# Reordering the opening of a two-block transformer kernel: the first token half ahead of the second, on one Trainium2 core

## Chip, cores and metric

The kernel runs on one core of one Trainium2 chip. The metric is the device time of one execution in microseconds (us), less is better. Engine names: PE is TensorE (matrix products; PEld its weight loads), DVE is VectorE, ACT is ScalarE, POOL is GpSimd, SP is SyncE, which issues most DMA transfers here.

## What is computed

Two blocks follow each other on x of 1024 tokens by 1024 channels, all in float32: a two-layer block (Fourier mixing and differential attention, then a short convolution, each with a modulated norm) and a second block (recurrent mixers and an MLP). Only the first modulated norm and the first projection bear on this change:

```python
m = jax.nn.silu(cvec) @ w + b
shift, scale, gate = jnp.split(m, 3, axis=-1)
h = rms_norm(x, g) * (1.0 + scale) + shift     # rms_norm: x / sqrt(mean(x*x) + 1e-6) * g
proj = h @ w_in
```

The rest of the reference (attention, convolutions, recurrences, the MLP) is the same work before and after.

## The kernel before

The program is written out by hand: one instruction list for each engine, tied together with semaphores, so each engine runs its instructions in the order written. Activations lie with channels on the 128 partitions, eight tiles of 128 channels (`k`), and 1024 tokens in the free dimension, which is handled as two halves of 512 (`h`). A projection unit is 128 output channels. Each product is made of three matmuls (high part by high, low part by high, high part by low): ACT rounds a weight tile to its high part (`Whi`, line 475), POOL subtracts to get the low part (`Wlo`, line 403), and PE multiplies.

The opening does the following.

- SP loads the parameters, then `x` as eight tiles of 512 KB (line 332: four for half 0, four for half 1), weight unit 0, two tiles of the modulation matrix `adaW` of 1 MB each (line 340), weight unit 1, then the other `adaW` tiles.
- ACT squares the 16 tiles of `x` (line 532), DVE adds them in fours (lines 1011, 1013, `add_fours`), PE sums over channels with a matrix of ones (line 1576), ACT takes the root (line 536), DVE inverts it (line 980, `root_to_scale`), giving `Rx` for each half.
- PE multiplies `silu(c)` by pairs of `adaW` tiles (line 1582, `modulation_rows(j)`, j from 0 to 3), ACT copies the result to `mrow` (line 540, `rows_out`), PE turns it into columns (line 1603, `modulation_columns(j)`), and DVE makes of them the shift `M` and the scale `A0` of two channel tiles (lines 990 to 995, its own `modulation_columns(j)`).
- For each channel tile and half, DVE makes the scaled tile `tnx` (line 1000, `scaled_half`), ACT adds the shift and rounds to the high part `Hh` (line 545, `high_half`), DVE makes the low part `Hl` (line 1005, `low_half`), and PE adds the tile's products to two units at once (lines 1614 to 1616, `first_products`: six matmuls a half).

On PE the order is: four sum matmuls, rows 0, columns 0, then for j = 1 to 3 the products of one half tile, rows j, one half tile, columns j, two half tiles, and at the end the last four half tiles. After that come the context's square sum (line 1637), the second pair of weights, and the projections that fill most of the kernel (lines 1489 to 1491).

Of the kernel before, what the change touches and what calls it, by code (L numbers as in the profile page):

```python
# [17 lines left out]
P = 128  # L18
# [4 lines left out]
KT = D // P  # L23
# [86 lines left out]
def build(nc, I, out_dram):  # L110
    names = {}

    def sem(name):
        if name not in names:
            names[name] = nc.alloc_semaphore(name)
        return names[name]
# [4 lines left out]
    def at(name, offset, shape, dt=F32):  # L121
        return nc.alloc_sbuf_tensor_at(name, [P] + list(shape), dt, offset=base + offset)
# [142 lines left out]
    def bank(b, n=512, off=0):  # L265
        return PS[:, b * 512 + off:b * 512 + off + n]
# [38 lines left out]
    def sp_program(sp):  # L305
# [20 lines left out]
        sp.dma_start(P12[:, :], nW["params"]).then_inc(sem("params_loaded"), 16)  # L326
        sp.dma_start(basic[:, :], nW["basic"]).then_inc(sem("const_loaded"), 16)
        xk = nW["x"].rearrange("p (k n) -> p k n", k=KT)
        for h in range(2):
            c = slice(h * 512, h * 512 + 512)  # L330
            for j in range(4):
                sp.dma_start(X[:, 2 * j:2 * j + 2, c], xk[:, 2 * j:2 * j + 2, c]).then_inc(sem(f"x_loaded{h}{j}"), 16)
        unit_at(0, 0, w_in0)
        for t in range(8):
            if t == 2:
                unit_at(1, P, w_in0)
            col = 1024 * (t % 2) + 256 * (t // 2)
            if t >= 4:
                sp.wait_ge(sem("ada_read"), t - 3)
            sp.dma_start(adaW[:, t % 4, :, :], ada[:, 0, :, col:col + 256]).then_inc(sem(f"ada_loaded{t % 4}"), 16)  # L340
        sp.wait_ge(sem("xsq_read"), 3)
        sp.dma_start(Xc[:, :, :], nW["ctx"].rearrange("p (k n) -> p k n", k=KT)).then_inc(sem("ctx_loaded"), 16)
        for u in range(2, BASE["g"] + 3):
# [126 lines left out]
    def act_program(act):  # L470
        def split(u, slot, load, tiles=KT):

            act.wait_ge(w_loaded[slot], load)
            act.wait_ge(acc_ready, u + 1)
            act.activation(Whi[:, slot, 0:tiles, :], Wraw[:, slot, 0:tiles, :], COPY).then_inc(hi_ready, 1)  # L475
# [48 lines left out]
        act.activation(small[:, 32:40], small[:, 24:32], ACT.Exp, scale=-1.0).then_inc(sem("lam_exp"), 1)  # L524
        act.wait_ge(sem("lamsum"), 1)
        act.activation(small[:, 8:10], bank(0, 2), ACT.Exp).then_inc(sem("lamexp"), 1)
        for n in range(2 * KT):
            h, k = n // KT, n % KT
            act.wait_ge(sem(f"x_loaded{h}{k // 2}"), 16)
            if n == 12:  # L530
                act.wait_ge(sem("xsq_read"), 1)
            act.activation(xsq[:, n % 12, :], X[:, k, h * 512:h * 512 + 512], SQUARE).then_inc(sem("xsq_ready"), 1)
        split(0, 0, 16)
        for h in range(2):
            act.wait_ge(sem("xsq_read"), 2 * h + 2)
            act.activation(Rx[:, h * 512:h * 512 + 512], bank(4 + h), SQRT, bias=EPSC, scale=1.0 / D).then_inc(sem("x_root"), 1)

        def rows_out(j):
            act.wait_ge(sem("ada_psum"), 2 * j + 2)
            act.activation(mrow[:, :, :], PS[:, 6 * 512:8 * 512].rearrange("p (t n) -> p t n", t=2)[:, :, 0:256], COPY).then_inc(sem("m_copied"), 1)  # L540

        def high_half(n):
            k, c = n // 2, slice(n % 2 * 512, n % 2 * 512 + 512)
            act.wait_ge(sem("x_tn"), n + 1)
            act.activation(Hh[:, k, c], tnx[:, n % 4, :], IDN, bias=M[:, k, 0:1]).then_inc(sem("x_hi"), 1)

        rows_out(0)
        split(1, 1, 16)
        act.dma_start(chan[:, :], nW["chan_dft"]).then_inc(sem("chan_loaded"), 16)
        for j in range(4):  # L550
            high_half(4 * j)
            high_half(4 * j + 1)
            if j < 3:
                rows_out(j + 1)
            high_half(4 * j + 2)
            high_half(4 * j + 3)
# [331 lines left out]
    def dve_program(dve):  # L888
# [88 lines left out]
        def root_to_scale(h):  # L977
            c = slice(h * 512, h * 512 + 512)
            dve.wait_ge(sem("x_root"), h + 1)
            dve.reciprocal(Rx[:, c], Rx[:, c])  # L980
            dve.drain()
# [14 lines left out]
            dve.drain().then_inc(sem("m_ready"), 1)  # L996

        def scaled_half(n):
            k, c = n // 2, slice(n % 2 * 512, n % 2 * 512 + 512)
            stt(tnx[:, n % 4, :], X[:, k, c], A0[:, k:k + 1], Rx[:, c], ALU.mult, ALU.mult).then_inc(sem("x_tn"), 1)  # L1000

        def low_half(n):
            k, c = n // 2, slice(n % 2 * 512, n % 2 * 512 + 512)
            dve.wait_ge(sem("x_hi"), n + 1)
            stt(Hl[:, k, c], tnx[:, n % 4, :], M[:, k, 0:1], Hh[:, k, c].bitcast(F32), ALU.add, ALU.subtract).then_inc(sem("x_lo"), 1)

        def add_fours(n):
            a = 4 * (n % 3)
            for b in (0, 2):
                dve.wait_ge(sem("xsq_ready"), 4 * n + b + 2)  # L1010
                tt(xsq[:, a + b, :], xsq[:, a + b, :], xsq[:, a + b + 1, :], ALU.add)
            dve.drain()
            tt(xsq[:, a, :], xsq[:, a, :], xsq[:, a + 2, :], ALU.add).then_inc(sem("xsq_added"), 1)

        for n in range(4):
            add_fours(n)
        root_to_scale(0)
        root_to_scale(1)
        modulation_columns(0)
        for j in range(4):  # L1020
# [9 lines left out]
            if j < 3:  # L1030
                modulation_columns(j + 1)
# [446 lines left out]
    def pe_program(pe):  # L1478
# [93 lines left out]
        for h in range(2):  # L1572
            for j in range(2):
                n = 2 * h + j
                pe.wait_ge(sem("xsq_added"), n + 1)
                mm(bank(4 + h), ones, xsq[:, 4 * (n % 3), :], start=(j == 0), stop=(j == 1)).then_inc(sem("xsq_read"), 1)

        def column_tiles(out, W, sem_done):

# [5 lines left out]
        def modulation_rows(j):  # L1585

            if j:
                pe.wait_ge(sem("m_copied"), j)
            for t in range(2):
                pe.wait_ge(sem(f"ada_loaded{(2 * j + t) % 4}"), 16 * (j // 2 + 1))  # L1590
                column_tiles(bank(6 + t, 256), adaW[:, (2 * j + t) % 4, :, :], "ada_psum")
                pe.drain().then_inc(sem("ada_read"), 1)

        def modulation_columns(j):

            pe.wait_ge(sem("m_copied"), j + 1)
            if j >= 2:
                pe.wait_ge(sem("m_ready"), j - 1)
            if j == 0:
                pe.wait_ge(sem("x_root"), 2)  # L1600
# [5 lines left out]
        def first_products(k, h):  # L1606

            pe.wait_ge(sem("x_lo"), 2 * k + h + 1)
            c = slice(h * 512, h * 512 + 512)
            for u in range(2):  # L1610
                if k == 0 and h == 0:
                    pe.wait_ge(lo_ready, u + 3)
                    pe.wait_ge(sem("lamexp"), 1)
                mm(acc(u)[:, c], Whi[:, u, k, :], Hh[:, k, c], start=(k == 0), stop=False)
                mm(acc(u)[:, c], Whi[:, u, k, :], Hl[:, k, c], start=False, stop=False)
                last = mm(acc(u)[:, c], Wlo[:, u, k, :], Hh[:, k, c], start=False, stop=(k == KT - 1))
                if k == KT - 1 and h == 1:
                    last.then_inc(acc_ready, 1)

        pe.wait_ge(sem("cs_ready"), 2)  # L1620
        modulation_rows(0)
        modulation_columns(0)
        for j in range(1, 4):
            first_products(2 * j - 2, 0)
            modulation_rows(j)
            first_products(2 * j - 2, 1)
            modulation_columns(j)
            first_products(2 * j - 1, 0)
            first_products(2 * j - 1, 1)
        for k in (6, 7):  # L1630
            for h in range(2):
                first_products(k, h)
        for k in range(KT):
            pe.wait_ge(sem("csq_ready"), k + 1)
            if k == 0:
# [463 lines left out]
```

## Time and profile before

| | |
|---|---|
| median of 3 runs | 2922.23 us (2921.93 to 2924.31) |
| profiled execution, its own time | 2921.74 us |
| span of its trace | 2919.9 us |
| PE busy | 2836.0 us, 97% of the span |
| DVE busy | 1436.9 us, 49% |
| ACT busy | 902.2 us, 31% |
| POOL busy | 636.3 us, 22% |

The span runs from the first to the last instruction; the execution's own time is 1.8 us longer. Starts in the trace are counted from the span's start. Of the span only about the first 45 us are in an order that the change touches.

### The profile page before, as it was taken

The numbers are of one execution on the slowest core, as the hardware profiler recorded it, in microseconds if no ns is written. First come the engines' busy times: TensorE is split into PE (matmuls) and PEld (weight loads), VectorE is DVE, ScalarE is ACT, GpSimd is POOL, SyncE is SP. The second block draws the span as 40 slices with busy tenths as digits, with TensorE's granted clock in tenths as the row PEclk, the third lists the DMA queues.
The fourth block names the chain that finished last, engine by engine and source line by source line (L and its number), as shares of the span: only waits on it lengthen the run. The fifth ranks groups of instructions, "written<-read, shape, count | busy, mean of one in ns | idle before, by whom it ended". The sixth has DMA issues, their size and how long they took to land.

```text
span 2919.9 us, 34652 instructions
## 1 busy us (share of the span) xinstructions
PE 2836.0 (97%) x14282; PEld 2360.1 (81%) x14282; DVE 1436.9 (49%) x1522; ACT 902.2 (31%) x1020; POOL 636.3 (22%) x348
## 2 busy tenths in 40 slices
PE   7999998899999999999999999999999999999997
PEld 4878777887788888788888888888877888888886
DVE  6478128877422226545555565655766213131236
ACT  4332226653211113444442222222333112121122
POOL 0111115214222213222221111111032121222222
PEclk9999999999999999999999999999999999999999
DMA  7211440023111112111111111111021111111113
GB/s 227 68 29 40 148 144 1 1 73 90 47 51 49 45 51 82 51 49 44 51 54 37 37 30 37 37 37 31 28 80 51 51 51 44 51 51 49 46 54 112
DMA packets 276868, 168.52 MB, mean 58 GB/s; under 512 B 5616, under 2 KB 270192, under 8 KB 276336
## 3 DMA queue, kind: packets, MB, share of 16 engines
q1 hardware_dynamic: 275280, 162.88, 19.0%
q10 hardware_dynamic: 1440, 3.51, 0.3%
q8 instruction: 113, 1.85, 0.3%
q14 instruction: 35, 0.29, 0.0%
HBM read 162.17 MB, written 4.19 MB: 57 GB/s over the span
## 4 chain that ended last, share of the span: by engine, by line
issue 52%; PE 36%; POOL 7%; DVE 2%; ACT 2%; DVEq 1%; POOLq 0%; ACTq 0%
PE PS L1489 10%; PE PS L1491 10%; PE PS L1490 10%; POOL Wlo L403 7%; ACT exp L677 1%; DVE acol L1159 1%; PE PS L1661 1%; DVEq L1163 1%; PE PS L1798 1%; PE PS L1582 1%; PE PS L1670 0%; PE PS L1801 0%; PE PS L1651 0%; PE PS L1681 0%; PE PS L1680 0%
## 5 line engine op out<-in xcount | busy, mean ns | idle before, releaser
L403 POOL TENSOR_TENSOR Wlo<-Wraw,Whi 128x1024 fp32r<-128x1024 f32 (+1 forms) x240 | 571.7, 2382 | 2113.2 <-ACT Whi L475 2113.2
L1489 PE MATMUL PS<-Bh,Whi 128*128 128x512 f32 x2176 | 860.6, 396 | 3.6 <-POOL Wlo L403 3.6
L1491 PE MATMUL PS<-Bh,Wlo 128*128 128x512 f32 x2176 | 849.6, 390 | 0.0
L1490 PE MATMUL PS<-Bl,Whi 128*128 128x512 f32 x2176 | 849.4, 390 | 0.0
L475 ACT ACTIVATE Whi<-Wraw 128x1024 fp32r<-128x1024 f32 (+1 forms) x240 | 250.4, 1043 | 781.5 <-PE PS L1491 779.1
L1489 PEld LDWEIGHTS PS<-Bh,Whi 128*128 128x128 f32 x2176 | 410.3, 189 | 91.8 <-POOL Wlo L403 6.5
L1491 PEld LDWEIGHTS PS<-Bh,Wlo 128*128 128x128 f32 x2176 | 409.9, 188 | 86.7
L1490 PEld LDWEIGHTS PS<-Bl,Whi 128*128 128x128 f32 x2176 | 410.3, 189 | 83.8 <-issue 1.5
L1489 PE MATMUL PS<-Hh,Whi 128*128 128x512 f32 x1120 | 444.8, 397 | 6.8 <-POOL Wlo L403 3.6
L1491 PE MATMUL PS<-Hh,Wlo 128*128 128x512 f32 x1120 | 437.5, 391 | 0.0
L1490 PE MATMUL PS<-Hl,Whi 128*128 128x512 f32 x1056 | 412.5, 391 | 0.0
L1489 PEld LDWEIGHTS PS<-Hh,Whi 128*128 128x128 f32 x1120 | 211.1, 188 | 59.1 <-issue 14.0
L1491 PEld LDWEIGHTS PS<-Hh,Wlo 128*128 128x128 f32 x1120 | 211.0, 188 | 44.5
L1490 PEld LDWEIGHTS PS<-Hl,Whi 128*128 128x128 f32 x1056 | 199.1, 189 | 42.0 <-issue 1.7
L1466 DVE TENSOR_TENSOR sq<-ut 128x1024 f32<-128x1024 f32 x32 | 83.7, 2616 | 197.0 <-ACT ut L880 197.0
L1473 DVE TENSOR_TENSOR X<-X,PS 128x1024 f32<-128x1024 f32 x24 | 29.3, 1221 | 214.3 <-PE PS L1491 214.3
L1933 PEld LDWEIGHTS PS<-hZ 128*128 128x128 f32 x896 | 108.8, 194 | 5.3 <-DVE hZ L1344 1.8
L1933 PE MATMUL PS<-hZ 128*128 128x64 f32 x896 | 107.8, 274 | 1.8 <-DVE hZ L1344 1.7
L1330 DVE COPY_PREDICATED hP<-mk,PS 128x512 f32<-128x512 int32 x56 | 50.1, 895 | 118.0 <-PE PS L1933 117.8
L677 ACT ACTIVATE exp<-PS,acol 128x1280 f32<-128x1280 f32 x60 | 79.6, 1327 | 60.3 <-DVE acol L1164 60.3
L910 DVE TENSOR_TENSOR sacc<-sacc,sqs 128x512 f32<-128x512 f32 x48 | 84.0, 1749 | 26.8 <-ACT sqs L494 26.8
L1825 PE MATMUL PS<-vT,probT 128*128 128x128 f32 x640 | 76.8, 275 | 0.0
(323 smaller groups left out, 3057.9 us busy)
## 6 DMA issues: line engine op xcount, KB each, us to landing
Wraw<-in_w_in SPq DMA_DIRECT2D x64, 512.0 KB, 4.1
Wraw<-in_w_down SPq DMA_DIRECT2D x38, 512.0 KB, 3.8
adaV<-in_ada_w SPq DMA_DIRECT2D x16, 1024.0 KB, 5.2
Wraw<-in_odd_w_in SPq DMA_DIRECT2D x32, 512.0 KB, 4.1
Wraw<-in_w_up SPq DMA_DIRECT2D x32, 512.0 KB, 4.1
Wraw<-in_even_w_in SPq DMA_DIRECT2D x24, 512.0 KB, 3.8
adaW<-in_ada_w SPq DMA_DIRECT2D x8, 1024.0 KB, 11.2
Wraw<-in_even_w_out SPq DMA_DIRECT2D x14, 512.0 KB, 3.8
```

The lines of the kernel that those rows point to most:

```text
L403: pool.tensor_tensor(Wlo[:, slot, 0:tiles, :], Wraw[:, slot, 0:tiles, :], Whi[:, slot, 0:tiles, :].bitcast(F32), ALU.subtract).then_inc(lo ...
L475: act.activation(Whi[:, slot, 0:tiles, :], Wraw[:, slot, 0:tiles, :], COPY).then_inc(hi_ready, 1)
L677: act.activation(weights_of(b, m)[:, :], PS[:, (S0, S1)[m]:(S0, S1)[m] + NK], ACT.Exp, bias=acol[:, b % 3, 5 + m:6 + m], accum_out=acol[:, ...
L910: tt(sacc[:, h, :], sacc[:, h, :], sqs[:, n % 2, :], ALU.add).then_inc(sem("sq_added"), 1)
L1330: dve.copy_predicated(hP[:, :].rearrange("p (c b two l) -> p c b two l", c=8, two=2, l=L)[:, :, :, 1, :], mk[lev][:, :].rearrange("p (a n) ...
L1466: tt(sq2[:, k % 2, :], ut[:, k % 2, :], ut[:, k % 2, :], ALU.mult).then_inc(sem("usq_ready"), 1)
L1473: tt(X[:, k, :], X[:, k, :], acc(k % 2), ALU.add).then_inc(acc_free[k % 2], 1)
L1489: mm(out, Whi[:, u % 2, k, :], hi[:, k, c], start=(k == 0), stop=False)
L1490: mm(out, Whi[:, u % 2, k, :], lo[:, k, c], start=False, stop=False)
L1491: return mm(out, Wlo[:, u % 2, k, :], hi[:, k, c], start=False, stop=(k == KT - 1))
L1825: ins = mm(rows_in(b), probT[:, b % 2, t, :], vT[:, t, h * P:(h + 1) * P], start=(t == 0), stop=(t == 9))
L1933: ins = mm(bank(4 + lev % 2, 64, c * 64).rearrange("p (b l) -> p b l", l=L), z, right, start=True, stop=True)
```

## The change

Tiles of `x` for half 0 are loaded first, then `adaW` tile 0, weight unit 0, `adaW` tile 1, weight unit 1, and only then half 1 of `x`. On ACT the root's table is loaded ahead of the squares by a root of one column whose result is not used, the squares of half 0 are followed by root 0, and the squares of half 1 stand behind the high parts of the first two tiles. On DVE and PE the sum, root and inversion of half 1 stand behind the first two half tiles, which are now channel tiles 0 and 1 of half 0 (`FIRST`) in place of both halves of tile 0. `modulation_rows(1)` stands behind half 1's sum, and `modulation_columns(1)` between the two half-1 tiles. The slots of the squares (`SQUARES_AT`) change so that those of half 1 do not meet `tnx`.

```diff
+    SQUARES_AT = (0, 4, 8, 4)
+    FIRST = [(0, 0), (1, 0), (0, 1), (1, 1)] + [(k, h) for k in range(2, KT) for h in range(2)]
...
-        unit_at(0, 0, w_in0)
-        for t in range(8):
-            if t == 2:
-                unit_at(1, P, w_in0)
+        x_half(0)
+        ada_tile(0)
+        unit_at(0, 0, w_in0)
+        ada_tile(1)
+        unit_at(1, P, w_in0)
+        x_half(1)
+        for t in range(2, 8):
+            ada_tile(t)
...
+        act.activation(small[:, 10:11], EPSC, SQRT)
...
+        for n in range(KT):
+            square(n)
+        x_root(0)
+        split(0, 0, 16)
         rows_out(0)
         split(1, 1, 16)
         act.dma_start(chan[:, :], nW["chan_dft"]).then_inc(sem("chan_loaded"), 16)
-        for j in range(4):
+        high_half(0)
+        high_half(1)
+        for n in range(KT, 2 * KT):
+            square(n)
+        x_root(1)
+        high_half(2)
+        rows_out(1)
+        high_half(3)
+        for j in range(1, 4):
...
-        for n in range(4):
-            add_fours(n)
+        add_fours(0)
+        add_fours(1)
         root_to_scale(0)
+        modulation_columns(0)
+        scaled_half(0)
+        scaled_half(1)
+        low_half(0)
+        low_half(1)
+        add_fours(2)
+        add_fours(3)
         root_to_scale(1)
-        modulation_columns(0)
-        for j in range(4):
+        scaled_half(2)
+        scaled_half(3)
+        low_half(2)
+        low_half(3)
+        for j in range(1, 4):
+            modulation_columns(j)
...
+        x_sum(0)
         modulation_rows(0)
         modulation_columns(0)
-        for j in range(1, 4):
-            first_products(2 * j - 2, 0)
+        first_products(0)
+        first_products(1)
+        x_sum(1)
+        modulation_rows(1)
+        first_products(2)
+        modulation_columns(1)
+        first_products(3)
+        for j in range(2, 4):
+            first_products(4 * j - 4)
             modulation_rows(j)
-            first_products(2 * j - 2, 1)
+            first_products(4 * j - 3)
             modulation_columns(j)
-            first_products(2 * j - 1, 0)
-            first_products(2 * j - 1, 1)
+            first_products(4 * j - 2)
+            first_products(4 * j - 1)
```

On PE, from the first six products on, this is the order before (`L1614` to `L1616` are products, `L1582` the `adaW` pieces, `L1603` the columns):

```order
L1614 MATMUL PS<-Hh,Whi 128x512 [waits lamexp,lo_ready]
L1615 MATMUL PS<-Hl,Whi 128x512
L1616 MATMUL PS<-Hh,Wlo 128x512
L1582 MATMUL PS<-adaW,cs 2x256 [waits ada_loaded2,m_copied]
L1582 MATMUL PS<-adaW,cs 2x256 x7
L1582 MATMUL PS<-adaW,cs 2x256 [waits ada_loaded3]
L1582 MATMUL PS<-adaW,cs 2x256 x7
L1614 MATMUL PS<-Hh,Whi 128x512 [waits x_lo]
L1615 MATMUL PS<-Hl,Whi 128x512
L1616 MATMUL PS<-Hh,Wlo 128x512
L1614 MATMUL PS<-Hh,Whi 128x512
```


and with the change, from the second half tile's products on (the same three product lines are now 1648 to 1650, the sum 1609, the `adaW` pieces 1615):

```order
L1648 MATMUL PS<-Hh,Whi 128x512
L1649 MATMUL PS<-Hl,Whi 128x512
L1650 MATMUL PS<-Hh,Wlo 128x512
L1609 MATMUL PS<-xsq,basic 128x512 [waits xsq_added] x2
L1615 MATMUL PS<-adaW,cs 2x256 [waits ada_loaded2,m_copied]
L1615 MATMUL PS<-adaW,cs 2x256 x7
L1615 MATMUL PS<-adaW,cs 2x256 [waits ada_loaded3]
L1615 MATMUL PS<-adaW,cs 2x256 x7
L1648 MATMUL PS<-Hh,Whi 128x512 [waits x_lo]
L1649 MATMUL PS<-Hl,Whi 128x512
L1650 MATMUL PS<-Hh,Wlo 128x512
```


Half 1's sum now stands between the second half tile and the `adaW` pieces of the second pair, so everything behind it on PE waits for half 1's squares and their additions.

On ACT, from half 1's squares on, the order before (line 532 squares, 536 roots, 540 the row copy, 475 the weights' high part, 545 `Hh`):

```order
L532 ACTIVATE xsq<-X 128x512 [waits x_loaded10] x2
L532 ACTIVATE xsq<-X 128x512 [waits x_loaded11] x2
L532 ACTIVATE xsq<-X 128x512 [waits xsq_read,x_loaded12]
L532 ACTIVATE xsq<-X 128x512 [waits x_loaded12]
L532 ACTIVATE xsq<-X 128x512 [waits x_loaded13] x2
L475 ACTIVATE Whi<-Wraw 128x1024 [waits acc_ready,w_loaded0]
L536 ACT_TABLE_LOAD
L536 ACTIVATE Rx<-PS,Dv 128x512 [waits xsq_read] x2
L540 ACTIVATE mrow<-PS 128x512 [waits ada_psum]
L475 ACTIVATE Whi<-Wraw 128x1024 [waits acc_ready,w_loaded1]
L549 DMA chan<-in_chan_dft 128x256
L545 ACTIVATE Hh<-tnx,M 128x512 [waits x_tn] x2
```


and with the change, from half 0's root on (now lines 543, 547, 551, 484 and 556):

```order
L547 ACTIVATE Rx<-PS,Dv 128x512 [waits xsq_read]
L484 ACTIVATE Whi<-Wraw 128x1024 [waits acc_ready,w_loaded0]
L551 ACTIVATE mrow<-PS 128x512 [waits ada_psum]
L484 ACTIVATE Whi<-Wraw 128x1024 [waits acc_ready,w_loaded1]
L564 DMA chan<-in_chan_dft 128x256
L556 ACTIVATE Hh<-tnx,M 128x512 [waits x_tn] x2
L543 ACTIVATE xsq<-X 128x512 [waits x_loaded10] x2
L543 ACTIVATE xsq<-X 128x512 [waits x_loaded11] x2
L543 ACTIVATE xsq<-X 128x512 [waits xsq_read,x_loaded12]
L543 ACTIVATE xsq<-X 128x512 [waits x_loaded12]
L543 ACTIVATE xsq<-X 128x512 [waits x_loaded13] x2
L547 ACTIVATE Rx<-PS,Dv 128x512 [waits xsq_read]
```


All eight squares of half 1 and its root now stand behind the first two `Hh` tiles, which wait for `tnx`; before, they stood ahead of the weights' high part and of both roots.

## Rows read from the trace of the kernel before

**Rows 1.** The page: span, and part 1, busy time of TensorE.

```profile
span 2919.9 us, 34652 instructions
...
PE 2836.0 (97%) x14282; PEld 2360.1 (81%) x14282; DVE 1436.9 (49%) x1522; ACT 902.2 (31%) x1020; POOL 636.3 (22%) x348
```

**Rows 2.** Timeline from 0 us, PE: start, duration, engine, line, operation, xcount, [idle before <-releaser].

```profile
18.70 2.08 PE L1576 MATMUL PS<-xsq,basic 128*128 128x512 f32 x2 [0.71 <-DVE xsq L1013]
...
20.87 1.89 PE L1582 MATMUL PS<-adaW,cs 128*2 128x256 f32 x16
...
23.84 1.89 PE L1582 MATMUL PS<-adaW,cs 128*2 128x256 f32 x16 [1.08 <-DMA adaW<-in_ada_w]
...
26.44 1.87 PE L1603 MATMUL PS<-P,mrow 128*128 128x2 f32 x8 [0.72 <-ACT mrow L540]
...
32.32 0.80 PE L1614 MATMUL PS<-Hh,Whi 128*128 128x512 f32 x1 [4.01 <-DVE Hl L1005]
...
35.18 3.33 PE L1582 MATMUL PS<-adaW,cs 128*2 128x256 f32 x32
...
38.66 0.49 PE L1614 MATMUL PS<-Hh,Whi 128*128 128x512 f32 x1
...
40.15 0.95 PE L1603 MATMUL PS<-P,mrow 128*128 128x2 f32 x8
...
44.18 0.50 PE L1614 MATMUL PS<-Hh,Whi 128*128 128x512 f32 x1 [0.20 <-DVE Hl L1005]
```

**Rows 3.** The same timeline, ACT.

```profile
6.18 0.17 ACT L526 ACTIVATE small<-PS 128x2 f32<-128x2 f32 x1 [0.60 <-PE PS L1571]
...
7.57 2.43 ACT L532 ACTIVATE xsq<-X 128x512 f32<-128x512 f32 x4 [0.18 <-DMA X<-in_x]
...
10.16 1.15 ACT L532 ACTIVATE xsq<-X 128x512 f32<-128x512 f32 x2 [0.17 <-DMA X<-in_x]
...
16.00 1.15 ACT L532 ACTIVATE xsq<-X 128x512 f32<-128x512 f32 x2 [0.28 <-DMA X<-in_x]
17.75 1.06 ACT L475 ACTIVATE Whi<-Wraw 128x1024 fp32r<-128x1024 f32 x1 [0.59 <-DMA Wraw<-in_even_w_in]
18.82 1.28 ACT L536 ACT_TABLE_LOAD   x1
...
20.11 1.39 ACT L536 ACTIVATE Rx<-PS,Dv 128x512 f32<-128x512 f32 x2
...
30.76 1.39 ACT L545 ACTIVATE Hh<-tnx,M 128x512 fp32r<-128x512 f32 x2 [3.43 <-DVE tnx L1000]
```

**Rows 4.** The same timeline, DVE.

```profile
20.83 6.78 DVE L980 RECIPROCAL Rx<-Rx 128x512 f32<-128x512 f32 x2 [2.19 <-ACT Rx L536]
...
28.35 0.16 DVE L990 TENSOR_TENSOR M<-PS,P 128x4 f32<-128x4 f32 x1 [0.73 <-PE PS L1603]
...
29.98 1.41 DVE L1000 SCALAR_TENSOR_TENSOR tnx<-X,Dv,Rx 128x512 f32<-128x512 f32 x2
...
41.16 0.15 DVE L990 TENSOR_TENSOR M<-PS,P 128x4 f32<-128x4 f32 x1
```

**Rows 5.** DMA issues from 20.76 to 23.6 us: KB, us from issue to landing.

```profile
adaW<-in_ada_w SPq DMA_DIRECT2D x1, 1024.0 KB, 11.2
```

**Rows 6.** Timeline from 50 us, PE: a later pass, and the end of the opening.

```profile
53.66 0.50 PE L1614 MATMUL PS<-Hh,Whi 128*128 128x512 f32 x1 [0.26 <-DVE Hl L1005]
...
74.68 0.47 PE L1489 MATMUL PS<-Hh,Whi 128*128 128x512 f32 x1 [2.33 <-POOL Wlo L403]
```

**Rows 7.** Windows, from 75.6 us, behind an idle time: busy times, then PEclk, DMA share, GB/s.

```profile
75.60:79.00 3.40, 3.40 (x10) 2.69 (x9) 3.32 (x6) 0.00 (x0) 2.13 (x1) 0.54 0.90 347
```

**Rows 8.** Windows: the stretch behind PE's longest idle time after 38 us.

```profile
444.98:448.40 3.42, 3.42 (x22) 2.32 (x23) 3.34 (x5) 2.02 (x2) 3.27 (x2) 1.00 0.00 0
```

**Rows 9.** Timeline of PE from 441 us: the idle time ahead of that stretch.

```profile
444.98 0.48 PE L1798 MATMUL PS<-kT,qT 64*128 64x256 f32 x1 [2.75 <-ACT exp L677]
```

**Rows 10.** Source line 1533 up to 700 us: ns of one, min/median/max, and starts.

```profile
L1533 PE MATMUL PS<-sacc,basic x2: 592/644/697, 697.4 to 697.9; 128*128 128x512 f32 x2
```

More of the change, by code:

```diff
@@ L328, in sp_program, with x_half @@
         xk = nW["x"].rearrange("p (k n) -> p k n", k=KT)
-        for h in range(2):
+        def x_half(h):
             c = slice(h * 512, h * 512 + 512)
@@ L332, in sp_program, with ada_tile @@
                 sp.dma_start(X[:, 2 * j:2 * j + 2, c], xk[:, 2 * j:2 * j + 2, c]).then_inc(sem(f"x_loaded{h}{j}"), 16)
-        unit_at(0, 0, w_in0)
-        for t in range(8):
-            if t == 2:
-                unit_at(1, P, w_in0)
+        def ada_tile(t):
             col = 1024 * (t % 2) + 256 * (t // 2)
@@ L526, in act_program, with square @@
         act.activation(small[:, 8:10], bank(0, 2), ACT.Exp).then_inc(sem("lamexp"), 1)
-        for n in range(2 * KT):
+        act.activation(small[:, 10:11], EPSC, SQRT)
+        def square(n):
             h, k = n // KT, n % KT
@@ L530, in act_program, with x_root @@
             if n == 12:
[L531 to L534, printed above, removed]
+                act.wait_ge(sem("xsq_read"), 2)
+            act.activation(xsq[:, SQUARES_AT[n // 4] + n % 4, :], X[:, k, h * 512:h * 512 + 512], SQUARE).then_inc(sem("xsq_ready"), 1)
+        def x_root(h):
             act.wait_ge(sem("xsq_read"), 2 * h + 2)
@@ L542, in high_half @@
         def high_half(n):
-            k, c = n // 2, slice(n % 2 * 512, n % 2 * 512 + 512)
+            k, c = FIRST[n][0], slice(FIRST[n][1] * 512, FIRST[n][1] * 512 + 512)
             act.wait_ge(sem("x_tn"), n + 1)
             act.activation(Hh[:, k, c], tnx[:, n % 4, :], IDN, bias=M[:, k, 0:1]).then_inc(sem("x_hi"), 1)
+        for n in range(KT):
+            square(n)
+        x_root(0)
+        split(0, 0, 16)
         rows_out(0)
@@ L998, in scaled_half @@
         def scaled_half(n):
-            k, c = n // 2, slice(n % 2 * 512, n % 2 * 512 + 512)
+            k, c = FIRST[n][0], slice(FIRST[n][1] * 512, FIRST[n][1] * 512 + 512)
             stt(tnx[:, n % 4, :], X[:, k, c], A0[:, k:k + 1], Rx[:, c], ALU.mult, ALU.mult).then_inc(sem("x_tn"), 1)
         def low_half(n):
-            k, c = n // 2, slice(n % 2 * 512, n % 2 * 512 + 512)
+            k, c = FIRST[n][0], slice(FIRST[n][1] * 512, FIRST[n][1] * 512 + 512)
             dve.wait_ge(sem("x_hi"), n + 1)
@@ L1007, in add_fours @@
         def add_fours(n):
-            a = 4 * (n % 3)
+            a = SQUARES_AT[n]
             for b in (0, 2):
@@ L1029, in dve_program @@
             low_half(n + 3)
-            if j < 3:
-                modulation_columns(j + 1)
         dve.wait_ge(sem("lam_exp"), 1)
@@ L1571, in pe_program, with x_sum @@
         mm(bank(0, 2), ones[0:64, :], small[0:64, 16:18], start=True, stop=True).then_inc(sem("lamsum"), 1)
-        for h in range(2):
+        def x_sum(h):
             for j in range(2):
@@ L1575, in pe_program @@
                 pe.wait_ge(sem("xsq_added"), n + 1)
-                mm(bank(4 + h), ones, xsq[:, 4 * (n % 3), :], start=(j == 0), stop=(j == 1)).then_inc(sem("xsq_read"), 1)
+                mm(bank(4 + h), ones, xsq[:, SQUARES_AT[n], :], start=(j == 0), stop=(j == 1)).then_inc(sem("xsq_read"), 1)
         def column_tiles(out, W, sem_done):
@@ L1598, in modulation_columns @@
                 pe.wait_ge(sem("m_ready"), j - 1)
-            if j == 0:
-                pe.wait_ge(sem("x_root"), 2)
+            if j < 2:
+                pe.wait_ge(sem("x_root"), j + 1)
             for t in range(2):
@@ L1604, in modulation_columns, with first_products @@
             ins.then_inc(sem("m_psum"), 1)
-        def first_products(k, h):
-            pe.wait_ge(sem("x_lo"), 2 * k + h + 1)
+        def first_products(n):
+            k, h = FIRST[n]
+            pe.wait_ge(sem("x_lo"), n + 1)
             c = slice(h * 512, h * 512 + 512)
@@ L1620, in pe_program @@
         pe.wait_ge(sem("cs_ready"), 2)
+        x_sum(0)
         modulation_rows(0)
         modulation_columns(0)
-        for j in range(1, 4):
-            first_products(2 * j - 2, 0)
+        first_products(0)
[7 more added lines that the diff above has]
+            first_products(4 * j - 4)
             modulation_rows(j)
-            first_products(2 * j - 2, 1)
+            first_products(4 * j - 3)
             modulation_columns(j)
-            first_products(2 * j - 1, 0)
-            first_products(2 * j - 1, 1)
-        for k in (6, 7):
-            for h in range(2):
-                first_products(k, h)
+            first_products(4 * j - 2)
+            first_products(4 * j - 1)
+        for n in range(12, 16):
+            first_products(n)
         for k in range(KT):
```

## Prediction

> **What bounds the kernel now.** Read the page first: PE is busy 2836.0 of 2919.9 us [rows 1], so the kernel ends when PE's list ends, and only PE's idle or slow time can be won. Then read the opening of the timeline. PE's first product stands at 32.32, after 4.01 us of idleness that ended with `Hl` [rows 2]. Followed back: `tnx` at 29.98 and the modulation columns at 28.35 [rows 4], the column turn at 26.44, and the second `adaW` tile, whose arrival at 23.84 ended a wait on DMA [rows 2]. So the first product hangs on that load. The inversions of both roots, 6.78 us from 20.83, end at 27.61, ahead of the columns at 28.35 [rows 4]: hidden. From 32.32 on PE is nearly gap free: two half tiles, `adaW` pieces and columns, up to the fifth half tile at 44.18, where it waited 0.20 us for `Hl` [rows 2]. The next like place is at 53.66 [rows 6], 9.48 us on, and the order from the fifth half tile on is unchanged. **So the change is worth what it moves that start from 44.18**; all behind it follows one for one, through the wait at 74.68 for POOL's `Wlo` [rows 6] too, since that tile's high part on ACT waits for the last product.
>
> **Part 1, loads.** Four `x` tiles are put behind the second `adaW` tile. ACT's squares start at 10.16 and 16.00 on the fourth and eighth tile's landing [rows 3]: 5.84 us of transfer. The second `adaW` tile then lands at 23.84 - 5.84 = 18.00. The bytes ahead of the third and fourth `adaW` tiles are the same as before, so the fourth still lands near 20.78 + 11.2 = 32 (issue and time to landing, [rows 5]); nothing later is late for its user.
>
> **Part 2, the first two half tiles.** The table load is moved ahead of the squares: 1.28 us [rows 3], from 6.35 (6.18 + 0.17) to 7.63, and a small root, about 0.1. Eight squares at 2.43 for four [rows 3] run from 7.75 to about 12.6; all their `x` has landed by 10.16. From the last square's end (16.00 + 1.15) to the last sum matmul at 18.70 it took 1.55 [rows 2, 3], so this sum starts at 14.15 and lasts 2.08 [rows 2], to 16.2. The first `adaW` tile's pieces follow, 1.89, to 18.15, so the second's start there and not at 18.00. The root (0.69) and one inversion (half of 6.78, 3.39) end near 20.4, hidden under this. The first product comes 8.48 us after the second `adaW` pieces (32.32 - 23.84), hence at **26.6; 5.7 us earlier than before**. The two `Hh` end at about 26.3 (32.15 before).
>
> What the trace shows of the table load: it lasts 1.28 us and the root starts at 20.11, 0.01 us behind its end, and the load itself starts straight after the work ahead of it [rows 3]. The Trainium skill, "ScalarE: Activation LUTs", section "What ACT_TABLE_LOAD costs", counts a drain of about 1380 ns more for every switch, 2.66 us in all. By that page the first sum and all behind it would come about 1.4 us later and the total would be 2927.8. The trace does not agree, and I use 1.28.
>
> **Part 3, the second half: a chain that was hidden.** Behind the second `Hh` (26.3) ACT makes eight squares, 4.8 us (twice 2.43), to 31.1; 1.55 to the last sum matmul: not before 32.65. PE has meanwhile done two half tiles: six products took 2.86 us (32.32 to 35.18) while PE ran at half rate, and 1.49 (38.66 to 40.15) at full rate [rows 2]. Both now start before PE is at full rate: 2.86, then six more 0.43 apart, 2.6, to 32.0. A sum takes 2.08 at half rate [rows 2], and about 1.1 at full rate (its two pieces start 0.5 apart and take about 0.6, [rows 10]). The rate rose inside the `adaW` pass at 35.18, between 2.9 and 6.3 us after the first product (that pass took 3.33 for two tiles against 1.89 for one, [rows 2]). Counted from 26.6 that is by about 32, so I take the sums at full rate: second one done at **34.0**. Then, in series, with nothing to hide it: root 0.75 with its handover, inversion 3.39, and from the first `tnx` to the product 2.34 (29.98 to 32.32, [rows 2, 4]) and a handover: 40.55 for the third half tile's products. PE has only the second pair's `adaW` pieces to do in this time, some 2.3 us, and then stands idle for about 4.2 us. This wait is new.
>
> **Part 4, to the fifth half tile.** From the start of the third half tile to the DVE columns it is 2.50 us at full rate (38.66 to 41.16), and at half rate 2.86 + 1.91 (26.44 to 28.35) = 4.77 [rows 2, 4]. From those columns to the fifth half tile 3.02 (41.16 to 44.18). At half rate 40.55 + 4.77 + 3.02 = **48.35**, at full rate 46.05. Which? After an idle stretch of 2.33 us at 74.68 the granted clock is 0.54 for 3.4 us [rows 6, 7], that is, the lower level, 1.2 GHz, almost throughout. But after 2.75 us of idleness at 444.98 it stays 1.00 [rows 8, 9]. The idleness here is longer than either, 4.2, so I take half rate. The Trainium skill, "TensorE: Matmul & The Clock Gate", says that an idle PE falls back to half rate and that work brings it back; the trace agrees at 75.6 and shows at 445 that an idle stretch of 2.75 us can pass without it.
>
> **Sum.** 48.35 - 44.18 = **+4.2 us**. The gain of 5.7 us at the front is spent on a serial chain of half 1 (squares, additions, sum, root, inversion) that was hidden behind loads. Against the profiled execution, 2921.74 us (span 2919.9), that is 2925.9; the median shown is 0.5 higher, so **2926.4 us**. Edits at no cost: the new square slots (same operations), the channel order in `FIRST` (same sizes), the unused root (0.1 us, counted).
>
> About 0.2%, 5.8 us, is what a measurement of this kernel tells from no change. The forecast lies inside it.
>
> **Rivals.**
>
> *Full rate stays.* For it: 445 us. Against it: 75.6 us and a longer idle time. The sum is then 46.05 - 44.18 = +1.9 us, 2924.1. If the rate also rises earlier, in the first half tile, the sums end some 0.6 sooner, 2923.5. This decides the lower end of the range.
>
> *PE never reaches full rate before the fifth half tile* (slower by over 0.2%). Place: the products from 26.6 and the two sums. If the rate has not risen by 32, the sums take 2.08 each and are done at 36.1; the chain puts the third half tile at 42.6 and the fifth, at half rate, at 50.4: +6.2, 2928.4. It decides from the point where the sum matmuls of half 1 last 2 us instead of 1.1. For it: before, the work from 20.87 to 28.3 did not raise the rate, and half 1's second sum waits a little on DVE. Against it: the 5.4 us of unbroken products ahead of the sums.
>
> *Half 1 keeps pace with its loads* (faster). Its last `x` tile lands near 18.00 + 1.75 + 5.84 = 25.6 (a weight unit took from 16.00 to 17.75, [rows 3]). If its squares ran as the tiles land, one square, 1.55, a sum of 2.08, 0.75 and 3.39 would end at 34.0, the third half tile would start at 36.4 and the fifth at 36.4 + 2.50 + 3.02 = 41.9: -2.3, 2919.9. Even this does not pass 0.2%; that takes the whole 5.7 of the front, 2916.5. Against both: on ACT the squares of half 1 stand behind both `Hh`, and ACT takes nothing out of order.
>
> *A dearer table load.* If the moved load holds ACT for twice its 1.28 us, all behind it is 1.3 later: 2927.7. Against it: the root 0.01 us behind the load [rows 3].
>
> **How the numbers follow.** Forecast 0.55, full rate kept 0.23, never at full rate 0.10, half 1 keeps pace 0.05 (0.03 of it with the whole gain), a dearer load 0.04, other 0.03, of which 0.01 faster by over 0.2%. The range takes the forecast with its unknown (the rate may return in the middle of part 4, up to 0.8 less; landing and handover 0.7 either way), reaches to the full-rate case below and past the half-rate case above: 2922.8 to 2929.0. Slower by over 0.2% (above 2928.1) takes the half-rate case, 0.10; faster by over 0.2% the whole gain and 0.01 of the other, 0.04; the rest, 0.86, is within.
>
> **What would show it.** Right: the second `adaW` pieces start near 18.1 and the first product near 26.6; ACT's eight squares of half 1 run from 26.3 to 31; an inversion of 3.35 us on DVE from about 34.8 with PE idle behind its `adaW` pieces for about 4 us; the third half tile near 40.5 with products 0.43 apart, the fifth near 48. Wrong: PE idle for under 2 us there, a granted clock of 1.00 over 40 to 46, or a fifth half tile ahead of 44.2. If the later passes were not 9.48 us apart any more, the one-for-one argument would be wrong.

## The result, and the profile after

| | before | changed |
|---|---|---|
| median | 2921.99 us (14 runs, 2920.37 to 2924.39) | 2926.69 us (14 runs, 2923.61 to 2928.45) |
| ratio to before, 95% interval | | 1.0016 [1.0009, 1.0023] |
| profiled execution, own time | 2921.74 us | 2926.97 us |
| span | 2919.9 us | 2925.2 us |

The changed kernel is slower by 4.7 us, 0.16%; measured again on another occasion (`after_again` below) it was slower by 3.2 us. The forecast was 2926.4 us. The page of the changed kernel, its first line and PE's of part 1, answers to [rows 1]:

```profile
span 2925.2 us, 34654 instructions
...
PE 2835.2 (97%) x14282; PEld 2360.5 (81%) x14282; DVE 1438.8 (49%) x1522; ACT 902.1 (31%) x1021; POOL 637.6 (22%) x348
```

PE is busy as long as before (2835.2 against 2836.0 us) in a span 5.3 us longer. The total does not tell where PE was slower, though: the eight matmuls of the two sums took 8.3 us before, all at half rate, and 5.9 us now, half of them at full rate, which hides the slower products shown below. The timeline of the changed kernel, PE (start, duration, engine, line, operation, xcount, [idle before <-releaser]), answers to [rows 2, 6]; lines 1648 to 1650 are the first products (1614 to 1616 before), 1609 the sum, 1615 the `adaW` pieces, 1636 the column turn, 1521 the third unit's first product:

```profile
15.72 1.89 PE L1615 MATMUL PS<-adaW,cs 128*2 128x256 f32 x16
...
18.44 1.04 PE L1615 MATMUL PS<-adaW,cs 128*2 128x256 f32 x16 [0.83 <-DMA adaW<-in_ada_w]
...
26.23 0.80 PE L1648 MATMUL PS<-Hh,Whi 128*128 128x512 f32 x1 [4.92 <-DVE Hl L1028]
...
31.42 1.88 PE L1609 MATMUL PS<-xsq,basic 128*128 128x512 f32 x4
...
33.23 2.23 PE L1615 MATMUL PS<-adaW,cs 128*2 128x256 f32 x32
...
39.84 0.79 PE L1648 MATMUL PS<-Hh,Whi 128*128 128x512 f32 x1 [4.38 <-DVE Hl L1028]
...
42.56 1.70 PE L1636 MATMUL PS<-P,mrow 128*128 128x2 f32 x8
...
47.32 0.80 PE L1648 MATMUL PS<-Hh,Whi 128*128 128x512 f32 x1 [0.29 <-DVE Hl L1028]
...
57.27 0.50 PE L1648 MATMUL PS<-Hh,Whi 128*128 128x512 f32 x1 [0.21 <-DVE Hl L1028]
...
78.28 0.47 PE L1521 MATMUL PS<-Hh,Whi 128*128 128x512 f32 x1 [2.33 <-POOL Wlo L412]
```

The first product starts at 26.23, 6.09 us earlier than before (32.32). The third half tile waits 4.38 us for `Hl` and starts at 39.84, the fifth at 47.32 (44.18 before), the ninth at 57.27 (53.66), the third unit at 78.28 (74.68). So a lead of 6.1 us has become a lag of 3.1 within 21 us, and 3.6 from the ninth half tile on, where it stays. The same timeline for ACT and DVE, which answers to [rows 3, 4]:

```profile
6.52 1.28 ACT L536 ACT_TABLE_LOAD   x1
...
7.81 0.20 ACT L536 ACTIVATE small<-Dv 128x1 f32<-128x1 f32 x1
...
24.67 1.39 ACT L556 ACTIVATE Hh<-tnx,M 128x512 fp32r<-128x512 f32 x2 [3.42 <-DVE tnx L1023]
...
25.96 4.25 ACT L543 ACTIVATE xsq<-X 128x512 f32<-128x512 f32 x8
...
31.02 0.69 DVE L1036 TENSOR_TENSOR xsq<-xsq 128x512 f32<-128x512 f32 x1
...
33.34 0.69 ACT L547 ACTIVATE Rx<-PS,Dv 128x512 f32<-128x512 f32 x1 [3.12 <-PE PS L1609]
...
34.06 3.35 DVE L1003 RECIPROCAL Rx<-Rx 128x512 f32<-128x512 f32 x1 [2.35 <-ACT Rx L547]
...
44.30 0.16 DVE L1013 TENSOR_TENSOR M<-PS,P 128x4 f32<-128x4 f32 x1 [3.43 <-PE PS L1636]
```

Here the chain of half 1 can be read as a staircase: second `Hh` done at 26.06 (24.67 + 1.39), eight squares from 25.96 to 30.21, last addition from 31.02 to 31.71, sum done at 33.30, root at 33.34, inversion from 34.06 to 37.41, third half tile at 39.84. Up to the sum two things run side by side, this chain and PE's own twelve products of the first two half tiles. In this profile PE's products ended last: it went into its four sum matmuls (31.42 to 33.30) without any idle time, and the pair that needs the last addition started near 32.28, 0.57 us behind that addition. So the squares were not what set the sum here, but they were close. From the root on the chain stands alone. PE's last work ahead of that, the `adaW` pieces, ended at 35.46. Windows of the changed kernel over PE's full-rate stretch and the one behind it (busy times of PE, PEld, DVE, ACT, POOL, then PEclk, DMA share, GB/s):

```profile
31.30:38.13 6.83, 4.02 (x37) 1.29 (x36) 4.41 (x3) 0.69 (x1) 0.00 (x0) 1.00 1.10 348
38.13:48.37 10.24, 8.24 (x23) 6.37 (x24) 6.00 (x13) 3.20 (x5) 0.00 (x0) 0.50 1.10 350
```

The granted clock is 1.00 (2.4 GHz) up to 38.13 and 0.50 (1.2 GHz) to 48.37. It fell while PE stood idle, and the full rate came back 8.5 us after PE's work had resumed.

For the experiments below, the start of the third unit's first product is the measure of the opening; everything that the change touches lies ahead of it. In the profiled executions it is 74.68 before, 78.28 changed.

### The profile page after: what moved, and what is told of

It is laid out like the page before. It is cut to its first block, busy times and chain, and to the rows that moved or that the text cites. A ratio compares the mean times of both kernels' runs of the same rounds, so it can differ in the third digit from the quotient of the medians.

```text
span 2925.2 us, 34654 instructions
## 1 busy us (share of the span) xinstructions
PE 2835.2 (97%) x14282; PEld 2360.5 (81%) x14282; DVE 1438.8 (49%) x1522; ACT 902.1 (31%) x1021; POOL 637.6 (22%) x348
## 3 DMA queue, kind: packets, MB, share of 16 engines
q8 instruction: 113, 1.85, 0.3%
## 4 chain that ended last, share of the span: by engine, by line
issue 52%; PE 36%; POOL 7%; DVE 2%; ACT 2%; DVEq 1%; POOLq 0%; ACTq 0%
PE PS L1521 10%; PE PS L1522 10%; PE PS L1523 10%; POOL Wlo L412 7%; ACT exp L700 1%; DVE acol L1191 1%; PE PS L1702 1%; DVEq L1195 1%; PE PS L1839 1%; PE PS L1615 1%; PE PS L1711 0%; PE PS L1842 0%; PE PS L1692 0%; PE PS L1722 0%; PE PS L1721 0%
```

## The experiments

**The two parts of the change, one at a time.** First the new order of loads in the kernel before (in short form):

```diff
-        x_half(0); x_half(1); unit_at(0); ada_tile(0); ada_tile(1); unit_at(1)
+        x_half(0); ada_tile(0); unit_at(0); ada_tile(1); unit_at(1); x_half(1)
```

> The kernel before with the new order of loads alone. Theory: half 1's x now lands near 26, the old order needs both halves' sums before the adaW rows, so the last sum ends near 30.8 instead of 20.8, the first product starts near 41 instead of 32.3, and the kernel is about 9 us slower than before, 2931. Rival (the first product hangs on the second adaW tile alone): it starts near 26.5 and the kernel is 5.8 us faster than before, 2916.

Measured: 2929.29 us median, ratio to before 1.0026 [1.0016, 1.0036]. Its PE timeline (1583 the sum, 1621 the first product of a half tile):

```profile
25.46 2.07 PE L1583 MATMUL PS<-xsq,basic 128*128 128x512 f32 x2 [10.26 <-DVE xsq L1020]
...
28.19 2.07 PE L1583 MATMUL PS<-xsq,basic 128*128 128x512 f32 x2 [0.65 <-DVE xsq L1020]
...
40.70 0.79 PE L1621 MATMUL PS<-Hh,Whi 128*128 128x512 f32 x1 [4.82 <-DVE Hl L1012]
...
51.89 0.50 PE L1621 MATMUL PS<-Hh,Whi 128*128 128x512 f32 x1 [0.20 <-DVE Hl L1012]
```

The last sum starts at 28.19 instead of 18.70, the first product at 40.70 instead of 32.32, the fifth half tile at 51.89, the third unit at 82.39: 7.7 us late. The theory held; the rival, that the first product hangs on `adaW` alone, fell.

Then the new order of ACT, DVE and PE with the old loads (in short form):

```diff
-        x_half(0); ada_tile(0); unit_at(0); ada_tile(1); unit_at(1); x_half(1)
+        x_half(0); x_half(1); unit_at(0); ada_tile(0); ada_tile(1); unit_at(1)
```

> The changed kernel with the old order of loads: the order of ACT, DVE and PE alone. Theory: the first product stays at 32.1 to 32.3 (its adaW tile lands near 23.8), half 1's chain starts only behind the second Hh tile near 32, so the third half tile starts near 45.7 and the fifth near 53: about 9 us slower than before, 2931. Rival (the lateness comes from half 1's x landing late, not from its squares' place): with x there early the third half tile starts by 40 and the kernel is at 2925 or less.

Measured: 2931.29 us, ratio 1.0034 [1.0023, 1.0045]. Its PE timeline:

```profile
23.74 1.89 PE L1615 MATMUL PS<-adaW,cs 128*2 128x256 f32 x16 [1.18 <-DMA adaW<-in_ada_w]
...
32.23 0.80 PE L1648 MATMUL PS<-Hh,Whi 128*128 128x512 f32 x1 [4.01 <-DVE Hl L1028]
...
45.53 0.79 PE L1648 MATMUL PS<-Hh,Whi 128*128 128x512 f32 x1 [4.38 <-DVE Hl L1028]
...
53.02 0.79 PE L1648 MATMUL PS<-Hh,Whi 128*128 128x512 f32 x1 [0.29 <-DVE Hl L1028]
```

First product 32.23, third half tile 45.53, fifth 53.02, third unit 83.88: 9.2 us late. The eight squares of half 1 start at 31.95 on ACT, straight behind the second `Hh`, while with the same order of loads in the kernel before the last `x` tile ended ACT's wait at 16.00: the squares are late by their place in ACT's list and not by late data. That place is not shown to be what costs the time, however. PE came to the sum of half 1 by its own list only at 37.12, behind the products of two half tiles, and ran its four matmuls in 1.88 us without a wait, as in the changed kernel. What the run shows is the price of the new order as a whole; no run moves the squares without the sum. The loads give the new order 5.6 us (83.88 against 78.28), and the new order costs 9.2: the difference is the 3.6 of the change. Each part alone costs more (7.7 and 9.2 us) than both together.

**The inversion taken out of half 1's chain.** This kernel leaves out a step of the computation: half 1 is scaled by the root and not by its inverse.

```diff
-            dve.reciprocal(Rx[:, c], Rx[:, c])
+            if h == 0:
+                dve.reciprocal(Rx[:, c], Rx[:, c])
```

> The changed kernel without the inversion of the root for token half 1 (3.35 us on DVE; the second half is then scaled by the root itself). Theory (squares, additions, sum, root and inversion of half 1 stand in series and set the third half tile): it starts 3.35 us earlier, near 36.5, PE's idle time falls from 4.38 to about 1 us, the rate stays full, and the fifth half tile starts near 42.0: 2921.4, about 5.3 us less than the changed kernel. Rival (adaW tiles or PE's own work hold the third half tile): it stays near 39 and the time within 1 us of 2926.7.

Measured: 2918.66 us, ratio 0.9989 [0.9979, 0.9998]. Its PE timeline at the third and fifth half tiles:

```profile
35.97 0.50 PE L1649 MATMUL PS<-Hh,Whi 128*128 128x512 f32 x1 [1.02 <-DVE Hl L1029]
...
41.48 0.50 PE L1649 MATMUL PS<-Hh,Whi 128*128 128x512 f32 x1 [1.55 <-DVE Hl L1029]
```

The third half tile starts 3.87 us earlier than in the changed kernel: 3.35 from the inversion, the rest because its sums started 0.51 us earlier (30.91 against 31.42). Its first product was only 0.09 us earlier and its last addition too (31.62 against 31.71); the rate rose within the second half tile's products, earlier than in the changed kernel, and so PE came to the sums sooner. The fifth starts at 41.48, expected 42.0, its products at full rate, and the third unit at 72.00: 6.3 us less than in the changed kernel, more than the inversion itself. The inversion is on the path to the third half tile, and behind the shorter wait (1.02 us) the products ran at full rate. The total came out 2.7 us under the 2921.4 expected: the stretch from the third unit to PE's next wait took 24.96 us here and 26.59 in the changed kernel, of which more below.

**PE kept busy in its idle time.** The wait is left as it is, only the rate is changed:

```diff
         modulation_rows(1)
+        for i in range(6):
+            mm(bank(4, 384, 128), ident, basic[:, :], start=True, stop=True)
         first_products(2)
```

> The changed kernel with six extra products of a constant tile (384 columns each, result never read) on PE in its idle time of 4.38 us ahead of the third half tile's products. Theory (of the changed kernel's lateness, the part above some 2 us is PE at half rate after that idle time): the third half tile still starts near 39.8, but its products come 0.23 us apart and not 0.43, the fifth half tile starts near 45.4 in place of 47.32, and the kernel is about 2 us faster than the changed one, 2924.7. Rival (the rate plays no part, the chain alone sets the fifth half tile): 47.3 and 2926.7.

Measured: 2922.39 us, ratio 1.0002 [0.9992, 1.0011]. PE's timeline (1663 is the added product) and the window from 31.3 to 80 us:

```profile
35.73 4.13 PE L1663 MATMUL PS<-basic 128*128 128x384 f32 x12
...
39.97 0.50 PE L1648 MATMUL PS<-Hh,Whi 128*128 128x512 f32 x1
...
45.47 0.50 PE L1648 MATMUL PS<-Hh,Whi 128*128 128x512 f32 x1 [1.55 <-DVE Hl L1028]
```

```profile
31.30:80.00 48.70, 43.41 (x256) 29.21 (x255) 32.87 (x73) 18.84 (x31) 4.74 (x2) 1.00 0.55 181
```

The third half tile starts at 39.97, no earlier than before; the clock stays at 1.00, and the fifth starts at 45.47, 1.85 us earlier (1.9 expected). It now waits 1.55 us for `Hl`, since at full rate PE is ahead of the chain columns, `tnx`, `Hh`, `Hl`. The third unit starts at 76.02, 2.26 earlier. So of the 3.6 us some 1.3 are the wait and 2.3 the half rate that follows from it. The median fell by more, 4.3 us: the stretch behind the third unit's start was shorter too, 24.95 us (76.02 to 100.97) against 26.59 (78.28 to 104.87), because the clock was not halved behind the idle time of 2.33 us there. That is not shown to be the work of the added products: in `no_inversion` and `columns_early` it was not halved there either, in `fill_gap`, where PE was busy too, it was. The attention stage differs as told below.

**The table load put back behind the squares of half 0.**

```diff
-        act.activation(small[:, 10:11], EPSC, SQRT)
```

> The changed kernel without the early root of one column, so the table is loaded between half 0's squares and its root. Theory (the table load costs 1.28 us and nothing besides, and the path to the first product goes over the second adaW tile): the squares start 1.4 us earlier but end with the loads, 0.5 us earlier, the table is loaded while ACT waits for the sum, and the first product stays within 0.3 us of 26.23. Rival (a drain of 1.4 us belongs to each load): the root starts over 2.6 us behind the last square and after the sum's end, and the early load had delayed the squares by 2.7 us.

One run: 2927.09 us, third unit at 78.24. ACT's timeline:

```profile
10.71 1.15 ACT L542 ACTIVATE xsq<-X 128x512 f32<-128x512 f32 x2 [0.22 <-DMA X<-in_x]
...
11.87 1.28 ACT L546 ACT_TABLE_LOAD   x1
...
15.52 0.69 ACT L546 ACTIVATE Rx<-PS,Dv 128x512 f32<-128x512 f32 x1 [2.37 <-PE PS L1608]
```

The last square ends 0.3 us earlier (11.86 against 12.17), the load takes 1.28 us inside ACT's wait for the sum, the root starts at 15.52 (15.83), and the first product at 26.37. Where the table load stands makes no difference here. It cost 1.28 us in both places, and in the changed kernel the root behind it started 0.01 us after its end (6.52 + 1.28, 7.81 above), so nothing of the length of a drain was seen.

**The changed kernel once more.**

> The changed kernel once more, on the same chip as the three above. In the first look the opening was 3.6 us later and the whole span 5.3 us longer. If the other 1.7 us belong to the change, the stretch from 104.9 to 666.4 us (561.5 long, 558.9 before) is again 561 or longer; if they come from where idle times fall in the attention stage from run to run, it lies anywhere between 558.9 and 561.5.

Measured: 2925.05 us, ratio 1.0013 [1.0003, 1.0022]. Third unit at 77.58, span 2923.4. In the opening the third half tile started as before, but the clock fell only during its products, so the fifth came 0.35 us earlier:

```profile
39.86 0.50 PE L1648 MATMUL PS<-Hh,Whi 128*128 128x512 f32 x1 [4.37 <-DVE Hl L1028]
...
46.97 0.58 PE L1648 MATMUL PS<-Hh,Whi 128*128 128x512 f32 x1 [0.29 <-DVE Hl L1028]
```

The last addition ended at 32.14 here (31.45 + 0.69) and the pair of sum matmuls that needs it started at 32.2: this time the squares' side set the sum. The stretch in question lasted 558.93 us (104.14 to 663.07). Windows from 444 to 456 us, first of the first profile, then of this one:

```profile
444.00:456.00 12.00, 9.24 (x47) 6.29 (x44) 9.42 (x17) 6.71 (x9) 9.03 (x7) 0.72 0.00 1
```

```profile
444.00:456.00 12.00, 8.63 (x69) 7.13 (x67) 10.79 (x19) 9.02 (x12) 9.89 (x9) 1.00 0.00 1
```

The idle time of 2.76 us ahead of this stretch is the same in all kernels (2.75 to 2.76). In the first profile the clock was halved behind it (0.72 over the window), in this one not (1.00). Over the profiles, taken by how long the clock was halved there:

| clock halved behind the idle time near 445 us | length of the stretch to the unit near 660 us |
|---|---|
| not at all (before; changed, second profile; new order with the old loads) | 558.9, 558.9, 559.0 |
| 3.4 us (kept busy; new loads alone; split later, told below) | 560.6, 560.6, 560.5 |
| 6.8 us (changed, first profile; no inversion; gap filled; columns early; late table) | 561.5, 561.2, 561.4, 561.7, 561.5 |

The first profile's stretch was 2.6 us longer than before, and what lies behind it 0.9 us shorter, which makes the 1.7 us by which its span was longer than its opening explains. The second profile of the same kernel does not have the 2.6, so they are no fixed part of the change. Why one execution has the halved clock and another not was not settled, nor whether the change makes it more frequent.

**The gap filled with useful work.** The idle time has room for the second pair's columns and the third pair's `adaW` pieces (pairs 1 and 2 in the code, in short form):

```diff
 # ACT
         x_root(1)
-        high_half(2)
         rows_out(1)
-        high_half(3)
+        high_half(2); high_half(3)
+        rows_out(2)
 # DVE
         root_to_scale(1)
+        modulation_columns(1)
 # PE
         modulation_rows(1)
+        modulation_columns(1)
+        modulation_rows(2)
         first_products(2)
-        modulation_columns(1)
         first_products(3)
+        modulation_columns(2)
```

Further on, `modulation_rows(3)` stands behind the sixth half tile and `modulation_columns(3)` behind the eighth, and DVE keeps `tnx` two half tiles ahead throughout.

> The changed kernel with useful work moved into PE's idle time ahead of the third half tile: the row copy, the column turn and the DVE columns of pair 1 stand behind half 1's root and inversion and ahead of its first tnx, and the adaW pieces of pair 2 stand ahead of the third half tile's products; pair 3's rows follow the sixth half tile. Theory (the loss is idle time in a serial chain plus half rate behind it, and both go when PE has work there): the third half tile starts near 40.5 at full rate, the context's sum on PE starts near 65 where it is 68.7 before, the third unit's first product near 70.5 (74.68 before, 78.28 changed), and the kernel takes about 2918, 4 us less than before and 8 less than the changed one. Rival (DVE's pace of one half tile in 1.34 us plus the columns takes over): the gain is halved, 2920 or more.

Measured: 2916.07 us (11 runs), ratio to before 0.9981 [0.9972, 0.9990]. PE's timeline (1628 the column turn, 1607 the `adaW` pieces, 1640 a half tile's first product):

```profile
35.61 1.05 PE L1628 MATMUL PS<-P,mrow 128*128 128x2 f32 x8 [0.71 <-ACT mrow L551]
...
36.59 1.05 PE L1607 MATMUL PS<-adaW,cs 128*2 128x256 f32 x16
...
37.92 1.04 PE L1607 MATMUL PS<-adaW,cs 128*2 128x256 f32 x16 [0.28 <-DMA adaW<-in_ada_w]
...
39.95 0.50 PE L1640 MATMUL PS<-Hh,Whi 128*128 128x512 f32 x1 [0.98 <-DVE Hl L1026]
...
46.56 2.23 PE L1607 MATMUL PS<-adaW,cs 128*2 128x256 f32 x32
...
69.53 0.47 PE L1513 MATMUL PS<-Hh,Whi 128*128 128x512 f32 x1 [2.33 <-POOL Wlo L412]
```

The longest wait left ahead of the third half tile is 0.98 us, it starts at 39.95, no earlier than in the changed kernel, but the columns of one pair and the `adaW` pieces of the next are done and the rate is full. The third unit starts at 69.53: 5.2 us earlier than before and 8.8 earlier than changed. It is 5.7 us faster than the kernel before (2921.81 on the same chip) and 9.0 faster than the changed one (2925.05 there): faster than both, with a small but clear gain over the kernel before.

The columns alone, with the third pair's rows left where they are:

> The changed kernel with the row copy, column turn and DVE columns of pair 1 alone moved ahead of the third half tile; pair 2's adaW pieces stay behind the fifth. Theory: the third half tile starts 0.65 us later, near 40.5, idle time on PE is about 3 us in two pieces, and the fifth half tile follows the fourth directly: 45.9 at half rate or 43.3 at full rate, where it is 47.32 in the changed kernel and 44.18 before; the kernel takes 2922 to 2925. Rival (the columns were never on the path, only the rate counts): the fifth half tile stays above 47.

Measured: 2923.30 us, ratio 1.0005 [0.9996, 1.0014], third unit at 74.83.

```profile
39.95 0.74 PE L1650 MATMUL PS<-Hh,Whi 128*128 128x512 f32 x1 [3.28 <-DVE Hl L1028]
...
44.41 0.40 PE L1650 MATMUL PS<-Hh,Whi 128*128 128x512 f32 x1
...
45.89 2.23 PE L1617 MATMUL PS<-adaW,cs 128*2 128x256 f32 x32
```

The fifth half tile starts at 44.41, 2.9 us earlier than in the changed kernel, in spite of 3.28 us of idle time and half rate up to 43.5. It is also 1.1 us earlier than with PE kept busy (45.47), where the rate was full throughout and the columns stood in their old place. So the columns behind the third half tile were on the path. The kernel is then level with before (74.83 against 74.68), and the rest of the edits above, with the full rate that they kept, adds 5.3 us (74.83 to 69.53).

**POOL's subtraction moved away from DVE's scale.** This came out of the timelines: a DVE operation on two columns took 2.02 us. POOL's and DVE's rows of the changed kernel:

```profile
21.33 2.34 POOL L412 TENSOR_TENSOR Wlo<-Wraw,Whi 128x1024 fp32r<-128x1024 f32 x1 [1.43 <-ACT Whi L484]
...
21.66 2.02 DVE L1017 SCALAR_TENSOR_TENSOR Dv<-M,P 128x2 f32<-128x2 f32 x1
```

```diff
-        split(1, 1, 16)
         act.dma_start(chan[:, :], nW["chan_dft"]).then_inc(sem("chan_loaded"), 16)
         high_half(0)
         high_half(1)
+        split(1, 1, 16)
```

> The changed kernel with the high part of weight unit 1 on ACT moved behind the first two Hh tiles, so that POOL's subtraction for it (2.34 us) no longer lies beside DVE's scale and first tnx. In every look so far DVE's operation on line 1017 took as long as POOL's subtraction still ran (2.02 us in the changed kernel, 1.12 before) and 0.16 us elsewhere. Theory (DVE stands still while POOL subtracts, and this, not the adaW tile alone, sets the first tnx): line 1017 takes 0.16 us, the first tnx starts near 22.1 instead of 23.89 and the first product near 24.4 instead of 26.23; POOL's subtraction then lies near 25.4 and holds up DVE's additions or low parts there. Rival (chance of timing, or a wait on something else): line 1017 still takes about 2 us or the first tnx stays at 23.9.

One run, 2929.60 us, third unit at 81.01. DVE and POOL:

```profile
22.95 0.16 DVE L1017 SCALAR_TENSOR_TENSOR Dv<-M,P 128x2 f32<-128x2 f32 x1
...
26.50 2.37 POOL L412 TENSOR_TENSOR Wlo<-Wraw,Whi 128x1024 fp32r<-128x1024 f32 x1 [6.49 <-ACT Whi L484]
...
27.50 2.52 DVE L1034 TENSOR_TENSOR xsq<-xsq 128x512 f32<-128x512 f32 x2 [1.23 <-ACT xsq L543]
```

Line 1017 takes 0.16 us, and two of DVE's additions beside POOL's subtraction now take 2.52 us together (0.69 each elsewhere). The theory of the standstill held; its numbers for the start did not: the second `adaW` tile came at 19.01 and the column turn ran at half rate, so `tnx` started at 23.31, not 22.1, and the first product at 25.66, not 24.4. The second unit's low part then held PE for 1.62 us at 28.92, and the opening got 2.7 us longer. Not a gain.

## Why the prediction was right, point by point

- *Loads.* The second `adaW` pieces started at 18.44, forecast 18.15. Right, but they started on the tile's landing (0.83 us of idle time on DMA), which was forecast at 18.00, and not behind the first pieces, which had ended at 17.61.
- *First product*, forecast 26.6, measured 26.23. The size is right, by errors that largely cancel: the start above was 0.3 us late, and two things within the 8.48 were off, together 0.7 us too long: the pieces and the column turn ran partly at full rate (1.04 and 1.12 us instead of 1.89 and 1.87), which I had not foreseen, and one DVE operation took 2.02 us beside POOL where I had carried along the 1.12 of before.
- *Table load.* 1.28 us at no cost to the path, as the rows of before said. The figure of the Trainium skill ("ScalarE: Activation LUTs", "What ACT_TABLE_LOAD costs"), 2.66 us with a drain, does not show in any run here.
- *Half 1's chain.* Squares 4.25 us instead of 4.8 (eight back to back take less than twice what four took before), sums done near 33.3 instead of 34.0, inversion 3.35, third half tile 39.84 instead of 40.55, idle time 4.38 instead of 4.2. Right in every step, 0.7 us too late in all. The 34.0 of the forecast was PE's own list, two sums behind two half tiles, with the squares' side some 0.3 us ahead of it (the last sum not before 32.65 by the squares, near 32.9 by PE's list: 34.0 less one sum of 1.1), and so it was: PE's list ended last in the first profile, the squares' side in the second. `no_inversion` shows the inversion on the path, `order_only` the price of the new order; that the squares' place in ACT's list costs anything by itself is not shown.
- *Rate behind the idle time.* Half rate, as taken: 4.46 us from the third half tile to the columns (39.84 to 44.30), forecast 4.77. The first rival, full rate kept, did not come about in either profile (in the second the first two products still ran at full rate); `keep_busy` shows what it would have given, a fifth half tile at 45.47 (forecast 46.05).
- *Fifth half tile*, forecast 48.35, measured 47.32: +3.1 us instead of +4.2. What was mis-sized are the small terms above. The passes behind it are one for one, but the first one took 9.95 us instead of 9.48, since the rate came back only at 48.37. From the ninth half tile to the third unit it is 21.01 us, 21.02 before: one for one.
- *The rival on the slower side* (never at full rate ahead of the fifth half tile) did not occur: the two sums took 1.88 us together, not 4.
- *The total.* The opening is 3.6 us later in the first profile and 2.9 in the second, forecast 4.2. The median came out at +4.7 (0.3 us from the forecast) the first time and at +3.2 the second. That the first is so close is partly luck: stretches that the change does not touch differ by up to 2.8 us between profiles in the attention stage alone (558.9 to 561.7).

## What to carry to other kernels

Starting one half earlier pays only if the other half's serial steps still run beside something. Look for what the old order hid (here above all the sum, the root and a 3.35 us inversion) and give the waiting engine, in its own list, the independent work that comes later anyway. A wait on PE can cost more than its length: here 1.3 us of net waiting brought 2.3 us of half rate, and products whose result nobody reads recovered the second part but not the first.

## What the runs showed of the hardware

- The same idle time of 2.33 us on PE ahead of the third unit was followed by about 3.4 us at granted clock 0.5 in seven of the eleven profiles, among them the kernel before and both of the changed one, and by none in four (PE kept busy, new loads alone, no inversion, columns early); the stretch to the next wait of PE is 26.6 us in the first case and 25.0 in the second. The 2.76 us near 445 were followed by 0, 3.4 or 6.8 us of it in three, three and five profiles.
- DVE operations with two SBUF operands stood still until POOL's subtraction ended (2.02 instead of 0.16 us, and 2.52 instead of 1.39 for two), while the inversion, which reads one, ran its 3.35 us beside POOL. The Trainium skill, "SBUF — State Buffer", "SBUF: two separate sides", describes this as a port pair that one of the two engines holds for a whole instruction; the runs agree.
